# Two blocks of two layers on one core: the first stage reordered, with half of the first w_ada tiles multiplied raw by TensorE

## The reference, cut to what matters

```
mod = silu(c) @ w_ada[l] + b_ada[l]              # c: 1024, w_ada: 1024 x 3072
shift, scale, gate = split(mod, 3)
h = rms_norm(x, norm_g[l]) * (1 + scale) + shift
z = h @ w_in[l]                                  # 1024 x 2976
c_q, c_kv, k_rope, g_mla, q_b, k_b, v_b, g_moba = split(z, ...)
o_mla  = mla_attention(c_q, c_kv, k_rope, ...)   # norms of c_q and c_kv, two more GEMMs, rope
o_moba = moba_attention(q_b, k_b, v_b, ...)      # norms of q and k by head, bias by distance
y = concat(silu(g_mla) * o_mla, silu(g_moba) * o_moba) @ w_out[l]
x = x + gate * y
```

## Time and profile before

| | |
|---|---|
| runs | 1740.73, 1738.62, 1740.21 us; median 1740.21 |
| profiled execution | 1740.04 us, span 1738.2 us |
| granted TensorE clock, mean | 0.98 |
| TensorE busy | 1618.8 us (93%) |
| VectorE busy | 1069.8 us (62%) |
| ScalarE busy | 845.4 us (49%) |
| GpSimd busy | 119.9 us (7%) |
| moved | 293.27 MB, mean 169 GB/s |

### The profile page before, as it was taken

One profiled execution on the slowest core, in us unless ns is written; L12 is line 12 of the kernel. 1 busy time (PEld: TensorE's weight loads), 2 busy tenths in 40 slices (PEclk: granted clock), 3 DMA queues, 4 the chain that ended last, 5 costly groups with the idle time before them and its releaser, 6 DMA issues.

```text
span 1738.2 us, 21793 instructions
## 1 busy us (share of the span) xinstructions
PE 1618.8 (93%) x7796; PEld 1326.2 (76%) x7796; DVE 1069.8 (62%) x1792; ACT 845.4 (49%) x1487; POOL 119.9 (7%) x157
## 2 busy tenths in 40 slices
PE   1778989999999999999999999999999999999998
PEld 1666777778888787877788887888778787778886
DVE  5786686666564546567665656565555556765553
ACT  0355546645444555555454445444455655454442
POOL 3011001100000300001100000000020000200000
PEclk9898989999999999999999999999999999999999
DMA  9674356336556553444555555555482353655552
GB/s 285 210 269 130 117 171 209 107 110 218 184 168 197 143 169 104 150 129 149 184 195 179 183 194 172 186 180 189 145 229 88 114 169 104 211 176 187 179 192 73
DMA packets 155336, 293.27 MB, mean 169 GB/s; under 512 B 10214, under 2 KB 23316, under 8 KB 155228
## 3 DMA queue, kind: packets, MB, share of 16 engines
q1 hardware_dynamic: 149312, 276.60, 49.1%
q0 software_dynamic: 4800, 12.29, 3.1%
q10 hardware_dynamic: 1116, 2.99, 0.5%
HBM read 290.77 MB, written 1.06 MB: 168 GB/s over the span
## 4 chain that ended last, share of the span: by engine, by line
PE 76%; DVE 9%; ACT 5%; issue 4%; DMA 4%; POOL 1%; SPq 0%; DVEq 0%; POOLq 0%; ACTq 0%
PE pb L434 72%; PE pb L438 4%; DMA raw<-in_w_in 2%; ACT wh L802 2%; DMA raw<-in_w_ada 2%; DVE acc L1284 2%; DVE wl L1287 2%; POOL st L2024 1%; ACT pb L802 1%; ACT p L802 1%; ACT xt_h L802 1%; DVE dg L1281 0%; DVE ti L1284 0%; DVE h L1284 0%; ACT ti L802 0%
## 5 line engine op out<-in xcount | busy, mean ns | idle before, releaser
L1287 DVE TENSOR_TENSOR wl<-raw,wh 128x1024 fp32r<-128x1024 f32 (+1 forms) x484 | 576.3, 1218 | 343.2 <-ACT wh L802 339.4
L802 ACT ACTIVATE wh<-raw 128x1024 fp32r<-128x1024 f32 (+1 forms) x484 | 496.3, 1051 | 267.9 <-PE pb L434 224.2
L434 PE MATMUL pb<-wh,xt_h 128*128 128x512 f32 (+2 forms) x1536 | 597.5, 389 | 13.5 <-ACT wh L802 11.5
L434 PE MATMUL pb<-wh,xt_l 128*128 128x512 f32 (+2 forms) x1536 | 589.6, 384 | 11.1 <-DVE xt_l L1284 11.1
L434 PE MATMUL pb<-wl,xt_h 128*128 128x512 f32 (+2 forms) x1536 | 588.2, 383 | 8.2 <-DVE wl L1287 8.0
L434 PEld LDWEIGHTS pb<-wh,xt_h 128*128 128x128 f32 x1536 | 294.6, 192 | 70.0 <-ACT xt_h L802 12.1
L434 PEld LDWEIGHTS pb<-wh,xt_l 128*128 128x128 f32 x1536 | 293.7, 191 | 70.3 <-DVE xt_l L1284 16.1
L434 PEld LDWEIGHTS pb<-wl,xt_h 128*128 128x128 f32 x1536 | 294.6, 192 | 61.4 <-DVE wl L1287 10.1
L434 PE MATMUL pb<-wh,big_h 128*128 128x512 f32 x352 | 140.2, 398 | 0.0
L434 PE MATMUL pb<-wh,big_l 128*128 128x512 f32 x352 | 139.6, 396 | 0.0
L434 PE MATMUL pb<-wl,big_h 128*128 128x512 f32 x352 | 139.5, 396 | 0.0
(11 more groups left out here) (206 smaller groups left out, 1485.3 us busy)
## 6 DMA issues: line engine op xcount, KB each, us to landing
raw<-in_ffn_w_gu SPq DMA_DIRECT2D x176, 512.0 KB, 4.6
raw<-in_w_in SPq DMA_DIRECT2D x148, 512.0 KB, 4.2
raw<-in_ffn_w_down SPq DMA_DIRECT2D x88, 512.0 KB, 3.7
raw<-in_w_ada SPq DMA_DIRECT2D x48, 512.0 KB, 5.4
raw<-in_w_out SPq DMA_DIRECT2D x32, 512.0 KB, 3.8
raw<-in_w_branch SPq DMA_DIRECT2D x24, 512.0 KB, 3.6
raw<-in_w_in SPq DMA_DIRECT2D x8, 416.0 KB, 4.1
G<-in_na_rpb POOLq DMA_DIRECT2D x32, 96.0 KB, 8.9
```

Of the source, the lines that this page charges most:

```text
L434: return e.matmul(o, a, b, start=start, stop=stop)
L802: return e.activation(o, a, func, **kw)
L1287: return e.tensor_tensor(o, a, b, op)
```

## The change

- Tiles 0 and 1 of layer 0 (shift) are weighed by VectorE as before. Tiles 2 and 3 (scale) go to TensorE raw: `ada_columns` multiplies a raw chunk by silu(c), eight float32 matrix calls of one column each, summed in PSUM bank 7 over the four chunks, behind one call that clears the bank. Each raw buffer is freed by TensorE's signal `row`. Chunks of the two kinds alternate in the queue.
- x is scaled, shifted and split in two halves of four blocks (`turn_x`), two blocks at a time, into `dg` and a buffer of attention. The first half needs tiles 0 and 2 only (`factors`). The first halves of the sums of z and qb (`part=0`) run on it; then come the raw chunks of tile 3, the second half of x, and the second halves (`part=1`). In layer 1 the order is: first half of x, half of z, second half of x, half of qb, the rest.
- One of the two row halves of x is normalised by ScalarE, the other by VectorE.
- The norms of z, qb and kb, the angles and `mbias` are ten steps spread over the ten chunks of the second half of qb, of kb and of vb. The squares of z are summed by ScalarE. The transposes for the latent GEMMs stand behind kb.
- w_ada's other tiles are spread by stage: none over z and qb, one over kb and vb, two over the six chunks from q0 on, two over gmoba's four, one over the output GEMM (layer 1: none, one, one, none). There are three accumulators, and `later` is filled ahead of `side`.
- ScalarE loads c and x first, then a table by a tanh that nobody reads, then tanh of c; `rows` follow this, the loads for the bias and `cst` the squares of x. GpSimd issues the `bc` broadcasts behind the powers of z.

```
 
     per = 1024 // n
     chunks = [(c0, min(per, nk - c0)) for c0 in range(0, nk, per)]
...
-    xtmp = [dg[:, 0:256], dg[:, 256:512]]
+    xtmp = [dg[:, :], pb1[2][:, :]]
...
     plan, split_at = [], []
-    first_tiles = [(0, j) for j in (0, 2, 1, 3)]
-    side_tiles = {(0, 0): [(1, 0), (1, 1), (1, 2), (0, 4), (0, 5)], (0, 1): [(1, 3)], (1, 0): [(1, 4), (1, 5)], (1, 1): []}
-    ada_tiles = first_tiles + [x for k in sorted(side_tiles) for x in side_tiles[k]]
...
+    side_tiles = {("kv", 0): [(1, 0)], ("lat", 0): [(1, 1), (1, 2)], ("gmoba", 0): [(0, 4), (0, 5)], ("out", 0): [(1, 3)],
+                  ("kv", 1): [], ("lat", 1): [(1, 4)], ("gmoba", 1): [(1, 5)], ("out", 1): []}
+    acc_tiles = [(0, 0), (0, 1)] + [x for k in side_tiles for x in side_tiles[k]]
+    acc_no = {x: i for i, x in enumerate(acc_tiles)}
+    acc = acc + [dg]
...
+        bank_of, kept = {}, {}
+
+        def take_early(g, src, n0, n, group):
+
+            wv = src.rearrange("(c p) n -> p c n", p=128)
+            for c0, kk in group:
+                kept[g, c0] = take(wv[:, c0:c0 + kk, n0:n0 + n], kk, n, ("mm", g, 1) if c0 + kk == wv.shape[1] else None)
+
...
+                         take(wv[:, c0:c0 + kk, n0:n0 + n], kk, n, ("mm", g, 1) if c0 + kk == nk else None)
                          for c0, kk in group]
...
+        def ada_columns(l, j, kq):
+
+            c = ada_chunk(l, j, kq)
+            v = chunk_view(raw[c % NRAW], c)
+            if kq == 0:
+                open_bank(7, ("mod", l, j))
+            w.wait_ge(*at("csil"))
+            if kq == 0:
+                w.wait_ge(*at("zero"))
+                mm(banks[7][:, 0:4], ident, stat(4, "zero"), True, False)
+            w.wait_ge(*at(f"raw{c % NRAW}", c))
+            for k in range(2):
+                kx = 2 * kq + k
+                for f in range(4):
+                    last = mm(banks[7][:, f:f + 1], v[:, k, f * 128:f * 128 + 128],
+                              stat(8, "c_silu")[:, kx:kx + 1], False, kx == 7 and f == 3)
+            last.then_inc(*up("row", l, j, kq))
+
...
+
+        def xkey0(t, kx):
+            return ("x", 0), kx | 1
+
+        win = d["w_in"][0]
+        for kq in range(4):
+            ada_chunk(0, 0, kq)
+            ada_columns(0, 2, kq)
+            if kq == 1:
+                b = rot("cols")
+                w.wait_ge(*at("rows"))
+                tr(b[:, 0:126], rows[0:126, :]).then_inc(*up("rtr"))
+            if kq == 2:
+                take_early(("z", 0), win, 0, 416, [(0, 2)])
+        take_early(("z", 0), win, 0, 416, [(2, 2)])
+        take_early(("qb", 0), win, 928, 512, [(0, 2), (2, 2)])
+        turn_row(0, 0)
+
+        def turn_x(l, c0):
+            to_xt(("x", l), lambda c, t: xn[:, t, c * 128:c * 128 + 128], c0 + 4, lambda c, t: [(f"xn{t}", l)], by="xm", c0=c0)
+
+        turn_x(0, 0)
+        gemm(("z", 0), XT, 0, xkey0, win, 0, 416, "eva", part=0)
+        gemm(("qb", 0), XT, 0, xkey0, win, 928, 512, "eva", part=0)
+        for kq in range(4):
+            ada_chunk(0, 1, kq)
+            ada_columns(0, 3, kq)
+            if kq == 1:
+                take_early(("z", 0), win, 0, 416, [(4, 2), (6, 2)])
+        take_early(("qb", 0), win, 928, 512, [(4, 2), (6, 2)])
+        turn_row(0, 1)
+        turn_x(0, 4)
 
         ps, pts = Ring(pb1), Ring(pt1)
         for l in range(NL):
...
+                later.drain()
+                later.add(ada(side_tiles[region, l]), 5 * len(side_tiles[region, l]))
+                later.over(chunks)
+
...
+                turn_x(l, 0)
+                gemm(("z", l), XT, 0, xkey, win, 0, 416, "eva", part=0)
+                turn_x(l, 4)
+                gemm(("qb", l), XT, 0, xkey, win, 928, 512, "eva", part=0)
+            gemm(("z", l), XT, 0, xkey, win, 0, 416, "eva", part=1)
             if l == 0:
                 b = rot("relb8")
...
+            gemm(("kb", l), XT, 0, xkey, win, 1440, 512, "eva")
             to_xt(("c", l), lambda c, t: z0[:, t, c * 128:c * 128 + 128], 3, lambda c, t: [("zn", l, t, 1)])
-            gemm(("kb", l), XT, 0, xkey, win, 1440, 512, "eva")
             gemm(("vb", l), XT, 0, xkey, win, 1952, 512, "eva")
+            more("lat", 6)
...
+
+        def load_rows(some):
+            for name, r0, n in some:
+                e.dma_start(rows[r0:r0 + n, :], d[name].rearrange("l (c p) -> (l c) p", p=128)).then_inc(
+                    *landed("c" if name == "c" else "rows"))
+
+        load_rows(rows_in[:1])
         e.dma_start(h[:, :, :], d["x"].rearrange("b (t p) n -> p (b t) n", p=128)).then_inc(*landed("x"))
+        w.wait_ge(*at("half"))
+        ac_(stat(1, "warm"), cols[:, 126:127], ACT.Tanh)
         rot()
         w.wait_ge(*at("ccol"))
         ac_(stat(8, "c_t"), cols[:, 0:8], ACT.Tanh, scale=0.5).then_inc(*up("ctanh"))
...
-        for _ in range(8):
-            next(first)
+        def rows_scale(l):
+            w.wait_ge(*at("rs", "rn", l, 1))
+            ac_(xn[:, 1, :], h[:, 1, :], scale=stat(1, "rs", "rn", l, 1)).then_inc(*up("xn1", l))
...
+        rows_scale(0)
+        split(stream.lead(9))
+        rot()
+        first = turn_x(0, 0)
+        next(first)
+        split(stream.lead(1))
+        next(first)
+        split(stream.lead(2))
+        split(stream.lead(10))
+        rot()
+        for _ in turn_x(0, 4):
+            pass
 
...
+
+            def norms():
+                for t in range(2):
+                    w.wait_ge(*at("eva", ("z", l), t))
+                    ac_(ob[:, t, 0:256], z0[:, t, 0:256], ACT.Square,
+                        accum_out=stat(1, "ss", "zq", l, t)).then_inc(*up("sq", "zq", l, t))
+                    ac_(ob[:, t, 256:384], z0[:, t, 256:384], ACT.Square,
+                        accum_out=stat(1, "ss", "zk", l, t)).then_inc(*up("sq", "zk", l, t))
+                yield
...
+                if l == 0:
+                    for at_, which, sign in ((0, 0, 1.0), (16, 0, 1.0), (32, 1, -1.0), (48, 1, 1.0)):
+                        w.wait_ge(*at("angle", which))
+                        ac_(rope[:, :, at_:at_ + 16], ang[:, 5 + which, :].rearrange("p (t f) -> p t f", t=2), ACT.Sin,
+                            scale=sign).then_inc(*up("sin", at_))
+                yield
+                yield
+                yield
...
+            at_ = row_of["b_ada"] + l * 24 + j * 4
+            w.wait_ge(*at("row", l, j, 3))
+            w.wait_ge(*at("cols"))
+            tt(mod[:, l, j * 4:j * 4 + 4], banks[7][:, 0:4], cols[:, at_:at_ + 4], ALU.add).then_inc(*up("mod", l, j))
+
...
+            w.wait_ge(*at("rs", "rn", l, 0))
+            ts(xn[:, 0, :], h[:, 0, :], stat(1, "rs", "rn", l, 0), None, ALU.mult, None).then_inc(*up("xn0", l))
+
+        def factors(l, z):
+
...
+            affine(*pairs_[1], 0)
+            lower(pairs_[0][0], pairs_[0][2])
+            yield
+            affine(*pairs_[1], 1)
+            lower(pairs_[1][0], pairs_[1][2])
+            yield
+
+        split(stream.lead(4))
...
+        rows_var(0)
+        split(stream.lead(2))
+        rows_scale(0)
+        split(stream.lead(3))
+        turn_row(0, 0)
+        columns(0, 2)
+        factors(0, 0)
+        first = turn_x(0, 0)
+        next(first)
+        split(stream.lead(1))
+        next(first)
+        split(stream.lead(2))
+        split(stream.lead(10))
+        turn_row(0, 1)
+        columns(0, 3)
+        factors(0, 1)
+        for _ in turn_x(0, 4):
+            pass
 
...
-                sum_squares(("zk", l, t), 1, 128, 128)
-                var(1, 256, ("zq", l, t), ("ss", "zq", l, t))
-                var(1, 128, ("zk", l, t), ("ss", "zk", l, t))
-            for t in range(2):
-                for i, (nm, a0, a1) in enumerate((("zq", 0, 256), ("zk", 256, 384))):
-                    w.wait_ge(*at("rs", nm, l, t))
-                    ts(z0[:, t, a0:a1], z0[:, t, a0:a1], stat(1, "rs", nm, l, t), None, ALU.mult, None).then_inc(
-                        *up("zn", l, t, i))
+                for z in range(2):
+                    factors(l, z)
+                rows_var(l)
+                rows_scale(l)
+                for _ in turn_x(l, 0):
...
                 for t in range(2):
-                    ts(ang[:, 0, t * 16:t * 16 + 16], cst[:, C_INV:C_INV + 16], stat(2, "pos")[:, t:t + 1], None,
-                       ALU.mult, None).then_inc(*up("ang0", t))
-                reduce_angle(0)
-                rot()
...
+                    reduce_angle(0)
+                yield
+                for t in range(2):
+                    for i, (nm, a0, a1) in enumerate((("zq", 0, 256), ("zk", 256, 384))):
+                        w.wait_ge(*at("rs", nm, l, t))
+                        ts(z0[:, t, a0:a1], z0[:, t, a0:a1], stat(1, "rs", nm, l, t), None, ALU.mult, None).then_inc(
+                            *up("zn", l, t, i))
+                yield
+                moba_var("qb", l)
+                yield
+                if l == 0:
+                    reduce_angle(1)
+                yield
```

(48 more changed lines are left out.)

295 lines of the change are left out of this document (151 added, 144 removed).

## The result

The changed kernel takes **1749.5 us** (median of five runs, 1747.2 to 1757.0) against 1739.6 for the kernel before, run beside it: a ratio of **1.0062, 95% interval 1.0041 to 1.0083**. It is slower by 0.6%, where 1.1% faster was forecast. The profiled execution is the longest of the five (1757.0, span 1755.2).

What follows compares the result with a forecast made beforehand. TensorE was taken as the bound, busy 93% of 1738.2 us, leaving only its 119 us of gaps to gain from. Terms -11.5 - 7.0 + 3.0 - 4.0 = -19.5 took 1740.0 to 1720.5 us, range 1711 to 1731.

Steps and rivals of the forecast that it cites:

- Part 1: Front of layer 0: the first half of z starts at 33 us instead of 59.7.
- rival (c): Front: a raw matrix call costs twice what the tile turns show, +9 and +5 us, giving 1734.5 us; 2%.
- Part 2: Layer 0 until qb is done: 72.6 us against 84.1 before, a term of -11.5 us.
- Part 3: kb and vb of layer 0: wait and slow clock go, a term of -7.0 us, bounds -8.5 and -3.
- I cost them at nothing, as the readers of both come two weight chunks later: kb and vb: ten bc issues on GpSimd's queue ahead of the bias transfer and qb powers add no time.
- 35 of 40 us: kb and vb: VectorE's forecast busy time between 60.2 and 100 us, called tight, with 1.5 us given back.
- Part 4: Attention stages of layer 0: 14 more weighings on VectorE cost +3 us, between 0 and 10.5.
- Part 5: Layer 1: the stop at z's middle and the slow restart go, a term of -4 us, bounds -2 and -5.
- (d): Attention: added weighings and their chunks' landings stand bare, +36 us in place of +3, giving 1753 us; 4%.
- (b): Worse handoff: late rows +3, slow raw chunks +2.5, VectorE behind in kb and vb +3, attention +2: 1731 us; 17%.
- (a): Quicker front: traffic hole closes -3, fast raw chunks -2.5, weighing hidden in attention -3: 1712 us; 14%.
- (e): No change: z to vb is limited by VectorE and transfers alone, early starts wait later: 1739 us; 3%.

Runs made afterwards that it cites:

- e6: Changed kernel with qb's first half multiplied behind the second turn of x instead of ahead of tile 3's raw chunks: 1749.1 us, 1.0058 of the kernel before.
- a0: The changed kernel run again unaltered, as yardstick and second profile: 1752.4 us, 1.0062 of the kernel before.
- e12: Changed kernel with the ten bc broadcasts issued behind the two bias transfers, still ahead of the qb powers: 1745.9 us, 1.0038 of the kernel before.
- e1: Changed kernel with the ten bc broadcasts issued behind the kb powers instead of ahead of the bias transfer: 1746.1 us, 1.0028 of the kernel before.
- e10: Changed kernel with weighing spread as before, bc broadcasts behind the kb powers, and weighing behind the attention step: 1722.9 us, 0.9892 of the kernel before.
- e13: e10 with the kb norm one step ahead of the second half of mbias: 1721.1 us, 0.9877 of the kernel before.
- e3: Changed kernel with VectorE weighing each chunk after that chunk's attention step instead of ahead of it: 1736.2 us, 0.9973 of the kernel before.
- e9: Changed kernel with VectorE's weighed tiles spread evenly over 22 weight chunks, as in the kernel before: 1736.1 us, 0.9964 of the kernel before.
- e2: Changed kernel multiplying only 8 of 512 columns of VectorE's tiles from the kb stage on, chunks still loaded: 1727.2 us, 0.9920 of the kernel before.
- e5: Changed kernel with layer 1's tiles 4 and 5 weighed over its kb and vb, none over its attention stages: 1742.4 us, 1.0010 of the kernel before.

## Why the prediction was wrong, by its steps

**Part 1 was right, and a little slow.** z starts at 30.4 where 33 was forecast. The last chunk that it needs is there at 22.4 where 24 was taken, and from 3 to 24 us the traffic never falls under 249 GB/s: the hole of the earlier trace rows is gone, with most of the gain of 2 to 3 us that was kept for the range. A raw chunk is 16 records. Two chunks right behind the half GEMMs take 4.16 us, near the fast price of 1.9 each; the last two take 6.99, the slow one of 3.6:

```profile
43.30 4.16 PE L439 MATMUL pb<-st,raw 128*128 128x1 f32 x32
...
49.08 6.99 PE L439 MATMUL pb<-st,raw 128*128 128x1 f32 x32 [1.62 <-DMA raw<-in_w_ada]
```

So rival (c) is out: the price in time is that of the earlier trace rows. The Trainium skill's four passes (FP8 and Floating Point Precision, TensorE Precision Notes) are not seen as records; what happens inside one, no run here shows.

**Part 2 was right.** Half GEMMs until 43.2 (44.4 forecast), a wait of 1.6 us for the third raw chunk but none for the fourth, the second half of z at 60.49 (60.2), qb done at 72.3 (72.6). Term: -11.8 for -11.5. Run e6 adds that 1.3 us gained at this place are gone by gmla.

**Part 3 failed in two steps.** The forecast was -7.0 with bounds -8.5 and -3; it is **+7.4** (+7.3 in a0), outside both. The first step that failed is "I cost them at nothing, as the readers of both come two weight chunks later". That counted 5.4 us of issue time on GpSimd's queue. Run e12 shows that this is indeed nearly free. What was not counted is that GpSimd waits for the bias to *land*, and that its 16 KB land late behind the broadcasts: 10.06 us where the kernel before waited 2.81. Whether the order within the queue or the load on the DMA engines delays them, no run tells apart. A moved DMA was priced as an instruction, and not as traffic ahead of a transfer that is waited for. It costs 6.3 us (e1). The second is "35 of 40 us" for VectorE. In the trace it is busy 8.35 + 33.20 = 41.6 us from 60.5 to 114.2, 6.2 more than the forecast's own terms give (35.4). 18 weighings stand there and not 14 (3.0 us). VectorE's part in the second turn of x (one scaling and two subtractions, 1.9) was not counted. The six splits fewer came (13 for 19), but save 5.9 us and not 7. In e10, where no wait for GpSimd is left, VectorE is busy 37.9 of 39.1 us and TensorE's 29 do not fill them. The order within the stage has a part too: the kb norm came last and TensorE waited 5.6 to 8.8 us for it (the two profiles and e1). Moving it ahead by one step brings q0 forward by 4.5 us but not the end (e13). So of the 14.4 us between forecast and measurement a run shows 6.3 (e1); how the rest divides between VectorE's sum and its order stays open.

**Part 4 failed in its price, and by its place.** The forecast was +3 with a bound of +10.5; it is **+16.0** (+11.7 in a0), and with 102.2 us (97.9) the two stages are past the 96 us that the forecast named as a sign of being wrong. The 10.5 was 14 weighings laid bare. The rests did not even come to that: TensorE's idle time in the two stages grew by 3.7 us (3.9 in a0), with 24 weighings there for 12, two fewer than forecast. The larger part, 12.3 us (7.8), is TensorE busy for longer, mostly at a lower clock: 0.77 and 0.90 in the two stages (0.85 and 0.90 in a0) against 0.91 and 1.00. The turn of one more tile is in it too (1.6 us). The upper bound left out the clock, though part 3 had counted it for its own stage, and the shares of idle VectorE (31% and 42%), by which the 3 was taken, say nothing of what stands ahead of what. Moving the same work behind the step wins 16 us over both layers (e3), spreading it as before wins 16 (e9), and weighing next to nothing wins 25 (e2).

**Part 5 was right, and what stood beside it was missed.** From z to q0 layer 1 takes 49.1 us for 52.6: -3.4, forecast -4 with bounds -2 and -5, and TensorE no longer stops at z's middle. But the diff also put tiles 4 and 5 of layer 1 into its two attention stages, where before they were spread over 26 chunks from z on. Part 4 counted layer 0 alone. That is +6.8 (3.2 of rests, the rest slower clock), and e5 takes it away with two entries of a table.

**The sum.** -11.8 + 7.4 + 16.0 for parts 1 to 4, -3.4 for layer 1's front and +6.8 for its attention stages make 15.0. The marks give 14.3 at the start of block 2, as 0.6 comes back in the output stage; 2.7 more pass behind it in the long profiled execution, where the two kernels are the same. In a0 the terms are -11.7, +7.3, +11.7, -3.6 and +7.6, together 11.3, and the marks give 10.7, close to the 9.9 us between the medians.

**The rivals.** (d) had the sign and the place, 1753 for 1749.5, with 4%. Its mechanism was half right and the nearness of its number is luck: the weighing ahead of a step costs, the landings of its chunks (25 of its 36 us) do not, since e2 loads all the chunks and is 25 us faster, and the clock, which it left out, filled their place. It was given too little because its price rested on the landings, which the profile spoke against, while the order, which every line of `take` shows, spoke for it. (b) had VectorE behind in kb and vb, with +3 where 14 were missing. (a) and (e) are out.

With the weighing spread as before and behind the steps, and the broadcasts behind the powers, the same first stage gives a kernel 18.8 us faster than the one before (e10), near the 19.5 that were forecast. Not all of that is the first stage: the spread alone leaves 5.6 (e9), and weighing behind the steps was not tried on the kernel before, which might gain by it too.

## What to carry to other kernels

A DMA that is moved on a queue has two prices, its issue and the landing of whatever is waited for behind it; look for a wait on a transfer further down that queue. Filler work on an engine that also carries the steps of a dependent chain belongs behind the step of its slot, not ahead of it, and idle share does not tell how much fits. An upper bound made of bare waits is too low where TensorE's clock can fall as well: in layer 1 3.2 us of added rests came with 3.5 to 4.3 us of the same instructions at a lower clock. And follow every tile that a table of placements moves, in all layers.

## What the runs showed of the hardware that was not expected

Small broadcasts are dear in DMA time. From 72 to 98 us the transfer views of a0 (first) and e1 (second) show GpSimd's queue (q0) and SyncE's (q1) with packets, MB and the share of the 16 engines:

```profile
q1 hardware_dynamic: 2719, 4.98, 53.1%
q0 software_dynamic: 648, 1.73, 39.9%
raw<-in_w_ada SPq DMA_DIRECT2D x4, 512.0 KB, 9.0
bias_scratch<-mk POOLq DMA_DIRECT2D x1, 16.0 KB, 9.7
```

```profile
q0 software_dynamic: 304, 1.07, 11.6%
raw<-in_w_ada SPq DMA_DIRECT2D x7, 512.0 KB, 4.6
```

The difference between the two, mainly the broadcasts, is 1.73 - 1.07 = 0.66 MB and 28% of all DMA time in that stretch, 43% for a megabyte, where q1 takes 10.7%. Chunks of w_ada beside them land in 9.0 us instead of 4.6. The Trainium skill (DMA: Bandwidth & Descriptors, Specifications) wants pieces of 512 B or more for full rate; of these packets only 136 more were under 512 B (352 for 216), so that this rule covers but a part of it. What makes them slow was not tried.
